# Cached latent attention of the sample group: four batches in four column tiles, and a page pool stored with its keys turned

## The chip, the core and the metric

The kernel is one program on one core of a Trainium2 chip. The number that counts is the device time of one execution in microseconds (us). TensorE (PE in the profile, PEld for its weight loads) multiplies, VectorE (DVE) and ScalarE (ACT) copy and reduce, GpSimd (POOL) and SyncE (SP) issue transfers here. An f32 matmul stands in the trace as two records, each with its own weight load.

## What is computed

One step of a two-layer decoder trunk for a prompt group (512 tokens) and a sample group (8 batches of 4 new tokens). The change is in the odd layer's latent attention of the sample group, which reads a paged cache of 16 pages of 128 keys for each batch:

```python
def mla_sample_attend(q_abs, q_pe, ckv, k_pe, pool_ckv, pool_kpe, page_table):
    past_ckv = pool_ckv[page_table].reshape(bd, past, c)          # 8 x 2048 x 256
    past_kpe = pool_kpe[page_table].reshape(bd, past, ROPE_DIM)   # 8 x 2048 x 32
    kc = jnp.concatenate([past_ckv, ckv], axis=1)
    kp = jnp.concatenate([past_kpe, k_pe], axis=1)
    sc = mla_scores(q_abs, q_pe, kc, kp)
    sc = jnp.where(kpos[None, :] <= qpos[:, None], sc, NEG)
    p = jax.nn.softmax(sc, axis=-1)
    return jnp.einsum('bhqj,bjc->bqhc', p.astype(kc.dtype), kc)
```

Each batch has 8 heads x 4 tokens = 32 query rows, so its scores are 32 rows by 2048 keys, with a contraction over 256 + 32 = 288 features.

## The kernel before

Most of the time goes to the dense panels (FFNs and projections, line 555), in each of which every weight panel is loaded by SP into `raw`, split by ACT and DVE into `w_hi` and `w_lo`, and multiplied. The order on each engine is written out by hand, with semaphores between them.

The odd layer runs its input panels, the prompt group's latent attention (`mla_score`, `mla_turn`, `mla_values`), then `sample()`, then `sample_out()` and the output panels (`mixer_out`). `mixer_out_begin` does the part of the first two output panels that needs no attention result; it stands behind the pages.

In `sample()` the 128 pages (8 batches x 16) go through TensorE one by one. A page arrives as 128 keys x 288 features (144 KB, `page_pool`). `turn_page` (line 862) turns it by three transposes against the identity, DVE and ACT copy the turned page from PSUM into `keys_t` in turns (lines 1608 and 1224), and `score_page` (line 875) multiplies it in three accumulating steps of 96 features with the stationary `qa` of that batch, 32 columns wide. Scores of batch b land in PSUM rows 32*(b%4) on, over banks 0 to 3. A score stands two pages behind its turn. Batch b-1's softmax runs beside batch b's pages: `sample_maxima` on DVE, four `Exp` on ACT (line 1232), `turn_probs` (line 906), and `page_values` (line 916), 16 accumulating matmuls of 256 columns against the pages as they came. The same loaded page serves both products.

`load_pages` issues the transfers: units of four pages, of which SP issues two of three and POOL the third. For each page the issuing engine reads the page number from the table (`value_load`, line 463), then issues one DMA (line 464). There are room and waits for 52 pages; the first 28 are loaded during the prompt group's attention.

## Time and profile before

| | us |
|---|---|
| median of 3 runs (lowest, highest) | 2413.91 (2412.71, 2418.8) |
| the profiled execution, span | 2412.8 |
| TensorE busy | 2344.1 (97%) |
| VectorE busy | 1085.6 (45%) |
| ScalarE busy | 754.7 (31%) |
| GpSimd busy | 232.4 (10%) |

The chain that ended last is 91% TensorE, of which 77% of the span is the panels' line 555, and lines 875 and 862, the page scores and page turns, are 4% and 2%. The span is the time from the first to the last instruction of one execution, so it can be set beside the median directly. In the views below, "x768" is a count of records, "idle before" is how long the engine had stood still, and the name behind "<-" is what it had waited for. The granted clock (PEclk) is 1.00 at 2.4 GHz and 0.50 at 1.2 GHz.

### The profile page before, as it was taken

What the parts mean: (1) busy time and instruction counts of PE and PEld (TensorE: products, weight loads), DVE (VectorE), ACT (ScalarE), POOL (GpSimd) and SP (SyncE); (2) the same over time, 40 slices, a digit from 0 to 9 for tenths busy, and PEclk for the clock granted to TensorE, in tenths of its full rate; (3) what the DMA queues carried; (4) which work ended last, traced back from release to release, by engine and by line L of the source; (5) the groups of instructions that cost most, each with busy time, mean ns of one, the idle gap of its engine ahead of it and who ended that gap; (6) DMA issues with size and microseconds to landing.
All of it is one profiled execution on the core that took longest, in us unless ns stands there. A gap on an engine that the chain in (4) does not pass through costs nothing.

```text
span 2412.8 us, 43405 instructions
## 1 busy us (share of the span) xinstructions
PE 2344.1 (97%) x17798; PEld 2200.5 (91%) x17798; DVE 1085.6 (45%) x1403; ACT 754.7 (31%) x1034; POOL 232.4 (10%) x201
## 2 busy tenths in 40 slices
PE   7999999998999999999999999988999989999997
PEld 7999999986999999999999999965666679999997
DVE  5432445455644244554334456664432345433443
ACT  5421222234344122244212222224422224522221
POOL 1001003000500000310000040400001021000002
PEclk9999999978999999999999999998999999999999
DMA  3243222320322222222222222232222112232222
GB/s 119 87 105 119 87 97 86 97 74 3 114 87 92 83 87 93 81 83 88 97 76 88 99 88 89 77 53 69 60 80 79 48 44 88 87 100 75 87 95 73
DMA packets 63131, 201.09 MB, mean 83 GB/s; under 512 B 8701, under 2 KB 20157, under 8 KB 62960
## 3 DMA queue, kind: packets, MB, share of 16 engines
q1 hardware_dynamic: 57776, 186.01, 23.8%
q0 software_dynamic: 5264, 13.79, 2.6%
q8 instruction: 66, 1.08, 0.2%
q14 instruction: 25, 0.20, 0.0%
HBM read 195.07 MB, written 5.71 MB: 83 GB/s over the span
## 4 chain that ended last, share of the span: by engine, by line
PE 91%; DVE 4%; ACT 2%; DMA 2%; issue 1%; DVEq 0%; SPq 0%; ACTq 0%
PE ps L555 77%; PE ps L875 4%; PE ps L862 2%; PE ps L916 2%; DMA raw<-down 1%; DMA raw<-w_uq 1%; DVE rinv L1288 1%; DVE w_lo L1278 1%; PE ps L791 1%; ACT prob L1093 1%; ACT p_mla L1190 0%; PE ps L643 0%; PE ps L804 0%; PE ps L642 0%; PE ps L906 0%
## 5 line engine op out<-in xcount | busy, mean ns | idle before, releaser
L555 PE MATMUL ps<-hx_hi,w_hi 128*128 128x272 f32 x3376 | 702.7, 289 | 15.5 <-DVE hx_lo L1299 13.1
L1026 ACT ACTIVATE w_hi<-raw 128x1024 fp32r<-128x1024 f32 (+2 forms) x299 | 334.6, 1119 | 1204.3 <-PE ps L555 1168.8
L555 PE MATMUL ps<-hx_hi,w_lo 128*128 128x272 f32 x3376 | 699.5, 289 | 0.0
L555 PE MATMUL ps<-hx_lo,w_hi 128*128 128x272 f32 x3376 | 696.9, 288 | 0.0
L555 PEld LDWEIGHTS ps<-hx_hi,w_hi 128*128 128x128 f32 x3376 | 531.7, 188 | 19.4 <-issue 14.3
L555 PEld LDWEIGHTS ps<-hx_lo,w_hi 128*128 128x128 f32 x3376 | 531.5, 189 | 0.0
L555 PEld LDWEIGHTS ps<-hx_hi,w_lo 128*128 128x128 f32 x3376 | 527.8, 189 | 0.0
L1278 DVE TENSOR_TENSOR w_lo<-raw,w_hi 128x1024 fp32r<-128x1024 f32 (+2 forms) x299 | 420.8, 1407 | 128.4 <-ACT w_hi L1026 128.1
L555 PE MATMUL ps<-hid_hi,w_hi 128*128 128x272 f32 x1408 | 291.9, 288 | 4.7 <-DVE w_lo L1278 4.7
L555 PE MATMUL ps<-hid_lo,w_hi 128*128 128x272 f32 x1408 | 291.6, 288 | 0.0
L555 PE MATMUL ps<-hid_hi,w_lo 128*128 128x272 f32 x1408 | 291.5, 288 | 0.0
L555 PEld LDWEIGHTS ps<-hid_hi,w_hi 128*128 128x128 f32 x1408 | 221.0, 189 | 4.9 <-issue 4.9
L555 PEld LDWEIGHTS ps<-hid_lo,w_hi 128*128 128x128 f32 x1408 | 221.0, 188 | 0.0
L555 PEld LDWEIGHTS ps<-hid_hi,w_lo 128*128 128x128 f32 x1408 | 220.9, 188 | 0.0
L1306 DVE SCALAR_TENSOR_TENSOR x<-ps,x 128x544 f32 (+1 forms) x80 | 57.9, 724 | 307.8 <-PE ps L555 307.8
L1323 DVE TENSOR_TENSOR up<-ps,rinv 128x544 f32<-128x544 f32 x88 | 63.8, 725 | 291.5 <-PE ps L555 291.5
L1320 DVE TENSOR_TENSOR gate<-ps,rinv 128x544 f32<-128x544 f32 x88 | 63.8, 725 | 232.8 <-PE ps L555 231.9
L1726 POOL TENSOR_TENSOR sumsq<-x 128x544 f32<-128x544 f32 x7 | 7.6, 1091 | 1337.5 <-DVE x L1306 1333.7
L1731 POOL TENSOR_TENSOR sumsq<-sumsq,square 128x544 f32<-128x544 f32 x49 | 113.0, 2306 | 3.8
L875 PE MATMUL ps<-keys_t,qa 96*32 96x128 f32 x768 | 107.5, 277 | 0.0
L875 PEld LDWEIGHTS ps<-keys_t,qa 96*32 96x32 f32 x768 | 73.7, 109 | 22.9 <-issue 22.9
L1608 DVE COPY keys_t<-ps 96x384 f32<-96x384 f32 x64 | 35.4, 554 | 103.7 <-PE ps L862 103.7
(280 smaller groups left out, 1955.8 us busy)
## 6 DMA issues: line engine op xcount, KB each, us to landing
raw<-gu SPq DMA_DIRECT2D x176, 512.0 KB, 3.4
raw<-down SPq DMA_DIRECT2D x64, 704.0 KB, 4.0
page<-page_pool SPq DMA_DIRECT2D x88, 144.0 KB, 2.5
raw<-odd_in SPq DMA_DIRECT2D x21, 512.0 KB, 3.4
raw<-even_in SPq DMA_DIRECT2D x14, 512.0 KB, 3.5
page<-page_pool POOLq DMA_DIRECT2D x40, 144.0 KB, 3.2
raw<-even_out SPq DMA_DIRECT2D x8, 512.0 KB, 3.4
raw<-odd_out SPq DMA_DIRECT2D x8, 512.0 KB, 3.5
```

The lines of the kernel that those rows point to most:

```text
L555: last = pe.matmul(acc[slot][0:m, a, 0:TH], w, r[:, t, a * TH:(a + 1) * TH], start=(begin and t == tiles[0] and one == 0), stop=(end and t ...
L791: pe.matmul(ps[:, i, 0:(i + 1) * P], qf[0:QK, h, i * P:(i + 1) * P], kf[0:QK, h, 0:(i + 1) * P], start=True, stop=True).then_inc(mla_score ...
L862: last = pe.transpose(ps[0:QK, page_bank[g], j * PAGE:(j + 1) * PAGE], pages[g % len(pages)][:, j * QK:(j + 1) * QK], ident[:])
L875: last = pe.matmul(ps_flat[r:r + NS, p * PAGE:(p + 1) * PAGE], qa[0:QK, j, b, :], keys_t[g % KT_SLOTS][:, j, :], start=(j == 0), stop=(j = ...
L916: pe.matmul(out, p_st[b % 2][:, p, :], pages[(b * PAGES + p) % len(pages)][:, 0:KV_LORA], start=(p == 0), stop=False)
L1026: act.activation(w_hi[slot][:, 0:cols], raw[slot][:, 0:cols], ACT.Copy).then_inc(w_hi_done, 1)
L1278: dve.tensor_tensor(w_lo[slot][:, 0:cols], raw[slot][:, 0:cols], w_hi[slot][:, 0:cols].bitcast(F32), ALU.subtract).then_inc(w_lo_done, 1)
L1306: dve.scalar_tensor_tensor(out=xm, in0=acc_of(slot), scalar=factor, in1=xm, op0=ALU.mult, op1=ALU.add)\
L1320: dve.tensor_tensor(halves(gate[:]), acc_of(n0 % 2), halves(rinv[:]), ALU.mult).then_inc(acc_read, 1)
L1323: dve.tensor_tensor(halves(up[:]), acc_of((n0 + 1) % 2), halves(rinv[:]), ALU.mult).then_inc(acc_read, 1)
L1608: dve.tensor_copy(keys_t[g % KT_SLOTS][:].rearrange("p j k -> p (j k)"), ps[0:QK, page_bank[g], 0:3 * PAGE])\
L1731: pool.tensor_tensor(sumsq[:], sumsq[:], square[:], ALU.add).then_inc(sumsq_step, 1)
```

## The change

The eight batches become two groups of four, and the four batches of a group are worked on together, batch b in column tile b (PSUM rows 32*b on).

- The pool is laid out twice. `pool_kt` holds each page with its features on the rows (96 rows of 3 x 128 elements, 144 KB), `pool_v` holds the latents as before without the rotary part (128 rows of 256 elements, 128 KB). The page table is stored in two orders to go with them.
- `turn_page` and the copies into `keys_t` are gone. `score_row(g, c)` multiplies four pages (512 keys) of each of four batches straight from `keys`: three feature steps, in each of which the four batches follow one another.
- `page_values(g)` takes one page of each of the four batches in turn, from `vals`. `score_new`, the masks, the maxima, the exponentials and `turn_probs` work on all 128 rows of a group at once.
- A unit is four pages: `load_keys` (32 units, all on SP, 8 slots) and `load_vals` (32 units, all on POOL, 9 slots). The four page numbers of a unit are read by one load. A slot of keys is free when its row of scores is done, a slot of values when its page is multiplied for all four batches. Two of the slots lie in `raw`, so SP loads the output panels from the third on only after the last page is used.
- `mixer_out_begin` moves from behind the pages to a place ahead of `page_values(1)`. Group 1's scores stand behind group 0's values.

```diff
+GROUPS = 2
+GB = DB // GROUPS
+ROWS = PAGES // 4
+K_SLOTS = 8
+V_SLOTS = 9
...
+        def page_numbers(eng, at):
+            return nc.values_load_multi_w_load_instructions(table[0:1, at:at + 4], engines=(eng.engine,), min_val=0, max_val=N_POOL - 1)[1]
+        def load_keys(eng, u):
+            if u == 0:
                 eng.wait_ge(table_landed, 16)
                 eng.wait_ge(q_done, HEADS)
                 eng.wait_ge(stored_conv, 32)
+            if u == 4:
+                eng.wait_ge(qa_done, 1)
+            if u == 6:
+                eng.wait_ge(w_lo_done, ODD_OUT + 2)
+            if u == 7:
                 eng.wait_ge(mla_scored, BLOCKS * HEADS)
+            if u >= K_SLOTS:
+                before = u - K_SLOTS
+                eng.wait_ge(scored[before % GB], before // (ROWS * GB) * (ROWS + 1) + before // GB % ROWS + 1)
+            for i, page in enumerate(page_numbers(eng, 4 * u)):
+                eng.dma_start(keys[u % K_SLOTS][:, i], d["pool_kt"][bass.ds(page, 1)].rearrange("a p j c -> (a p) j c"))\
+                   .then_inc(keys_landed[u % K_SLOTS], 16)
+        def load_vals(eng, u):
+            if u == 0:
+                eng.wait_ge(table_landed, 16)
+                eng.wait_ge(q_done, HEADS)
+            if u == 1:
+                eng.wait_ge(w_lo_done, ODD_OUT + 2)
+            if u == 2:
                 eng.wait_ge(qa_done, 1)
+                eng.wait_ge(mla_scored, BLOCKS * HEADS)
+            if u >= V_SLOTS:
+                before = u - V_SLOTS
+                for b in range(GB):
+                    eng.wait_ge(valued[b], before // PAGES * (PAGES + 1) + before % PAGES + 1)
+            for b, page in enumerate(page_numbers(eng, DB * PAGES + 4 * u)):
+                eng.dma_start(vals[u % V_SLOTS][:, b], d["pool_v"][bass.ds(page, 1)].rearrange("a p c -> (a p) c"))\
+                   .then_inc(vals_landed[u % V_SLOTS], 16)
...
+            for u in range(GROUPS * ROWS * GB):
+                load_keys(sp, u)
+            for b in range(GB):
+                sp.wait_ge(scored[b], GROUPS * (ROWS + 1))
+                sp.wait_ge(valued[b], GROUPS * (PAGES + 1))
...
+            def score_row(g, c):
+                if g == 0:
+                    pe.wait_ge(mla_exp, BLOCKS * HEADS)
+                else:
+                    pe.wait_ge(s_exp, c + 1)
+                for j in range(3):
+                    for b in range(GB):
+                        u = (g * ROWS + c) * GB + b
+                        if j == 0:
+                            pe.wait_ge(keys_landed[u % K_SLOTS], 64 * (u // K_SLOTS + 1))
+                        r = NS * b
+                        last = pe.matmul(ps[r:r + NS, c, :], qa[0:QK, j, g * GB + b, :], keys[u % K_SLOTS][:, :, j, :],
+                                         start=(j == 0), stop=(j == 2))
+                        if j == 2:
+                            last.then_inc(scored[b], 1)
+            def turn_probs(g):
+                for f in range(ROWS):
+                    pe.wait_ge(s_exp, g * (ROWS + 1) + f + 1)
+                    if f == 2 or f == 0 and g:
+                        pe.wait_ge(s_copied_act, 2 * g + f // 2)
+                    if f == 3 or f == 1 and g:
+                        pe.wait_ge(s_copied_dve, 3 * g + f // 2)
+                    for k in range(4):
+                        p = 4 * f + k
+                        last = pe.transpose(ps[:, 4 + f % 2, k * P:(k + 1) * P], p_s[:, p * PAGE:(p + 1) * PAGE], ident[:])
+                    last.then_inc(s_turned, 1)
+                pe.wait_ge(s_exp, (g + 1) * (ROWS + 1))
+                if g == 0:
                     pe.wait_ge(new_copied, 1)
                 else:
+                    pe.wait_ge(o_lat_done, g)
+                pe.transpose(ps[0:NS, 6, 0:P], p_s[:, PAGES * PAGE:PAGES * PAGE + NS], ident[:]).then_inc(s_turned, 1)
+            def page_values(g):
                 for p in range(PAGES):
+                    u = g * PAGES + p
+                    if p % 8 == 0:
+                        pe.wait_ge(s_copied_act, 2 * g + p // 8 + 1)
+                    if p % 8 == 4:
+                        pe.wait_ge(s_copied_dve, 3 * g + p // 8 + 1)
+                    pe.wait_ge(vals_landed[u % V_SLOTS], 64 * (u // V_SLOTS + 1))
+                    for b in range(GB):
+                        r = NS * b
+                        pe.matmul(ps[r:r + NS, 7, 0:KV_LORA], p_st[:, p, r:r + NS], vals[u % V_SLOTS][:, b, :], start=(p == 0), stop=False)\
+                          .then_inc(valued[b], 1)
+                pe.wait_ge(s_copied_dve, 3 * g + 3)
+                for b in range(GB):
+                    r = NS * b
+                    pe.matmul(ps[r:r + NS, 7, 0:KV_LORA], p_st2[:, r:r + NS], ckv_new[:], start=False, stop=True).then_inc(valued[b], 1)
             def sample():
+                turn_new()
+                for g in range(GROUPS):
+                    for c in range(ROWS):
+                        score_row(g, c)
+                    score_new(g)
+                    turn_probs(g)
+                    if g == GROUPS - 1:
+                        mixer_out_begin(ODD_OUT, CONV_TILES, CONV_PIECE + CT)
+                    page_values(g)
+                    turn_latents(g)
...
+                act.wait_ge(new_turned, 1)
+                act.activation(ckv_new[:], ps[0:NS, 6, 0:KV_LORA], ACT.Copy).then_inc(new_copied, 1)
+                for g in range(GROUPS):
+                    act.wait_ge(s_max, g + 1)
+                    if g:
+                        act.wait_ge(s_turned, g * (ROWS + 1))
+                    for c in range(ROWS):
+                        act.activation(p_s[:, c * 4 * PAGE:(c + 1) * 4 * PAGE], ps[:, c, :], ACT.Exp, bias=s_nmx[:, g:g + 1], scale=MLA_SCALE,
+                                       accum_out=s_sum[:, g, c:c + 1]).then_inc(s_exp, 1)
+                    act.activation(p_s[:, PAGES * PAGE:PAGES * PAGE + NS], s_new[:], ACT.Exp, bias=s_nmx[:, g:g + 1], scale=MLA_SCALE,
+                                   accum_out=s_sum[:, g, ROWS:ROWS + 1]).then_inc(s_exp, 1)
+                    if g:
+                        for b in range(GB):
+                            act.wait_ge(valued[b], g * (PAGES + 1))
+                    for f in (0, 2):
+                        act.wait_ge(s_turned, g * (ROWS + 1) + f + 1)
+                        act.activation(p_st[:, 4 * f:4 * f + 4, :].rearrange("p j r -> p (j r)"), ps[:, 4, :], ACT.Copy).then_inc(s_copied_act, 1)
...
+            def sample_maxima(g):
+                row = g * (ROWS + 1)
+                for c in range(ROWS):
+                    for b in range(GB):
+                        dve.wait_ge(scored[b], row + c + 1)
+                    dve.tensor_reduce(s_mx[:, g, c:c + 1], ps[:, c, :], AX, ALU.max)
+                for b in range(GB):
+                    dve.wait_ge(scored[b], row + ROWS + 1)
+                if g:
+                    dve.wait_ge(s_exp, row)
+                link(dve.tensor_tensor(s_new[:], ps[:, 7, KV_LORA:KV_LORA + NS], causal_s[:, g, :], ALU.add))
+                link(dve.tensor_reduce(s_mx[:, g, ROWS:ROWS + 1], s_new[:], AX, ALU.max))
+                link(dve.tensor_reduce(s_mx[:, g, ROWS + 1:ROWS + 2], s_mx[:, g, 0:ROWS + 1], AX, ALU.max))
+                dve.tensor_scalar(s_nmx[:, g:g + 1], s_mx[:, g, ROWS + 1:ROWS + 2], -MLA_SCALE, None, ALU.mult).then_inc(s_max, 1)
+            def sample_copies(g):
+                if g:
+                    for b in range(GB):
+                        dve.wait_ge(valued[b], g * (PAGES + 1))
+                for f in (1, 3):
+                    dve.wait_ge(s_turned, g * (ROWS + 1) + f + 1)
+                    dve.tensor_copy(p_st[:, 4 * f:4 * f + 4, :].rearrange("p j r -> p (j r)"), ps[:, 5, :]).then_inc(s_copied_dve, 1)
+                dve.wait_ge(s_turned, (g + 1) * (ROWS + 1))
+                dve.tensor_copy(p_st2[:], ps[0:NS, 6, 0:P]).then_inc(s_copied_dve, 1)
+            def sample_tokens(g):
+                for b in range(GB):
+                    dve.wait_ge(valued[b], (g + 1) * (PAGES + 1))
+                if g:
+                    dve.wait_ge(o_turned, g)
+                link(dve.tensor_reduce(s_rs[:, g, 0:1], s_sum[:, g, :], AX, ALU.add))
+                link(dve.reciprocal(s_rs[:, g, 1:2], s_rs[:, g, 0:1]))
+                dve.tensor_scalar(o_tok[:], ps[:, 7, 0:KV_LORA], s_rs[:, g, 1:2], None, ALU.mult).then_inc(o_tok_done, 1)
...
+            for u in range(GROUPS * PAGES):
+                load_vals(pool, u)
...
+    pool = np.concatenate([i["cache_mla_ckv"][0], i["cache_mla_kpe"][0]], -1)
+    a["pool_kt"] = pool.transpose(0, 2, 1).reshape(N_POOL, 3, QK, PAGE).transpose(0, 2, 1, 3)
+    a["pool_v"] = i["cache_mla_ckv"][0]
+    by_rows = i["page_table"].reshape(GROUPS, GB, ROWS, 4).transpose(0, 2, 1, 3)
+    by_pages = i["page_table"].reshape(GROUPS, GB, PAGES).transpose(0, 2, 1)
+    a["table"] = np.concatenate([by_rows.reshape(1, -1), by_pages.reshape(1, -1)], 1)
...```

**TensorE's order, scores.** Before, one period of one page in batch 2, with the score of a page two behind its turn (`page` is a page as loaded, `keys_t` a turned copy, `qa` the queries):

```order
L862 MATMUL ps<-ident_68,page33_182 96x128 [waits keys_copied0]
L862 MATMUL ps<-ident_68,page33_182 96x128 x2
L875 MATMUL ps<-keys_t1_170,qa_127 32x128 [waits keys_copied1]
L875 MATMUL ps<-keys_t1_170,qa_127 32x128 x2
L888 MATMUL ps<-ckv_115,qa_new_128 32x4 x2
L889 MATMUL ps<-kpe_116,qa_127 32x4
```

After, the first row of scores; a `keys` buffer holds four pages of one batch:

```order
L829 MATMUL ps<-ident_68,ckv_115 32x128 [waits mla_copied]
L829 MATMUL ps<-ident_68,ckv_115 32x128
L844 MATMUL ps<-keys0_146,qa_127 32x512 [waits keys_landed0,mla_exp]
L844 MATMUL ps<-keys1_147,qa_127 32x512 [waits keys_landed1]
L844 MATMUL ps<-keys2_150,qa_127 32x512 [waits keys_landed2]
L844 MATMUL ps<-keys3_145,qa_127 32x512 [waits keys_landed3]
L844 MATMUL ps<-keys0_146,qa_127 32x512
```

The transposes are gone, neighbouring matmuls are of different batches, and what they wait for is a transfer.

**TensorE's order, the end of the pages.** Before, the last values stand ahead of the output panels' first part:

```order
L916 MATMUL ps<-page22_163,p_st1_203 32x256
L916 MATMUL ps<-page23_164,p_st1_203 32x256
L917 MATMUL ps<-ckv_new_201,p_st2_176 32x256
...
L555 MATMUL ps<-mix_hi_72,w_hi1_57 128x272
L555 MATMUL ps<-mix_lo_73,w_hi1_57 128x272 x2
L555 MATMUL ps<-mix_hi_72,w_lo1_59 128x272 x2
...
L924 MATMUL ps<-ident_68,o_tok_175 128x128 [waits s_copied,o_tok_done]
```

After (`mix` and `w_hi` belong to the output panels):

```order
L879 MATMUL ps<-ident_68,p_s_163 32x128 [waits o_lat_done,s_exp]
L546 MATMUL ps<-mix_hi_72,w_hi1_57 128x272 [waits acc_read,w_lo_done,mix_done]
L546 MATMUL ps<-mix_hi_72,w_hi1_57 128x272
...
L892 MATMUL ps<-vals7_161,p_st_164 32x256 [waits vals_landed7,s_copied_act]
L892 MATMUL ps<-vals7_161,p_st_164 32x256 x3
...
L897 MATMUL ps<-ckv_new_165,p_st2_166 32x256 x3
L903 MATMUL ps<-ident_68,o_tok_149 128x128 [waits o_tok_done]
```

The panels' first part now stands between group 1's turned probabilities and its values.

**SP's order.** Before, one page has its own load of a page number; after, four pages share one, and the unit waits for a row of scores:

```order
L463 TENSOR_LOAD table [waits values_done]
L463 ISA x2
L464 ISA
L464 DMA page_177<-page_pool 128x288
L463 TENSOR_LOAD table
```

```order
L426 TENSOR_LOAD table [waits scored0]
L426 ISA x8
L444 ISA
L444 DMA keys_146<-pool_kt 96x384
L444 ISA
L444 DMA keys_146<-pool_kt 96x384
```

Three of four number loads are gone, and the wait comes every four pages.

## Rows read from the trace of the kernel before

**Rows 1.** Busy time by stretch: start:end, length, then each engine; clock, DMA, GB/s.

```profile
core 0: us, PE busy (x) PEld busy (x) DVE busy (x) ACT busy (x) POOL busy (x), PEclk, DMA share, GB/s
1711.00:1947.00 236.00, 230.58 (x1625) 151.56 (x1623) 67.38 (x151) 63.37 (x162) 13.41 (x25) 0.98 0.21 61
...
1704.00:1711.00 7.00, 3.85 (x21) 2.30 (x22) 2.74 (x9) 3.37 (x11) 3.22 (x6) 1.00 0.81 232
...
1937.00:1942.00 5.00, 4.67 (x11) 1.90 (x12) 0.00 (x0) 0.28 (x1) 0.00 (x0) 0.50 0.01 3
1943.00:1947.00 4.00, 4.00 (x20) 1.90 (x19) 0.00 (x0) 0.00 (x0) 0.00 (x0) 1.00 0.00 0
```

**Rows 2.** Groups by line and shape, 1706 to 1958: count, busy us, mean ns.

```profile
L875 PE MATMUL ps<-keys_t,qa 96*32 96x128 f32 x768 | 107.5, 277 | 0.0
...
L862 PE MATMUL ps<-ident,page 128*96 128x128 f32 x384 | 67.9, 286 | 0.3 <-DVE keys_t L1608 0.3
L916 PE MATMUL ps<-page,p_st 128*32 128x256 f32 x256 | 59.3, 392 | 0.8 <-ACT p_st L1242 0.8
...
L1573 DVE TENSOR_REDUCE mx<-ps 32x1 f32<-32x512 f32 x32 | 21.9, 685 | 2.4 <-PE ps L875 1.7
L1232 ACT ACTIVATE p_s<-ps,nmx 32x512 f32<-32x512 f32 x32 | 21.6, 675 | 5.7 <-DVE nmx L1583 5.3
```

**Rows 3.** TensorE in order of time, batch values and two pages: start, length.

```profile
1807.20 6.64 PE L916 MATMUL ps<-page,p_st 128*32 128x256 f32 x30
...
1815.55 0.53 PE L862 MATMUL ps<-ident,page 128*96 128x128 f32 x3
1816.01 0.84 PE L875 MATMUL ps<-keys_t,qa 96*32 96x128 f32 x6
1816.79 0.53 PE L862 MATMUL ps<-ident,page 128*96 128x128 f32 x3
```

**Rows 4.** TensorE in order of time, even layer, line 708, batches in four column tiles.

```profile
570.54 0.18 PEld L708 LDWEIGHTS ps<-k_cache,q_bd 128*32 128x32 f32 x8 [1.54 <-issue]
570.54 0.45 PE L708 MATMUL ps<-k_cache,q_bd 128*32 128x128 f32 x8
```

**Rows 5.** SP's and GpSimd's issues of pages; queue instructions: least/median/most ns.

```profile
1629.02 21.66 SPq L464 DMA_DIRECT2D page<-page_pool  x20
...
1705.46 0.54 POOL L464 DMA_DIRECT2D page<-page_pool  x1 [0.60 <-issue]
...
L463 SPq TENSOR_LOAD <-table x88: 262/269/487, 1628.0 to 1879.1; - x88
...
L463 POOLq TENSOR_LOAD <-table x40: 283/289/498, 1628.0 to 1874.7; - x40
```

**Rows 6.** DMA issues, 1640 to 1960: queue, count, KB, median us to landing.

```profile
page<-page_pool SPq DMA_DIRECT2D x78, 144.0 KB, 2.4
page<-page_pool POOLq DMA_DIRECT2D x32, 144.0 KB, 3.2
```

**Rows 7.** In order of time: prompt attention's end, batch 7's softmax, the tail.

```profile
1702.80 0.69 ACT L1190 ACTIVATE p_mla<-ps,nmx 128x512 f32<-128x512 f32 x1 [1.92 <-DVE nmx L1549]
...
1706.93 2.34 PE L815 MATMUL ps<-p_mla_t,v_mla 128*64 128x512 f32 x8 [0.78 <-ACT p_mla_t L1203]
...
1930.77 0.17 DVE L1580 TENSOR_TENSOR s_new<-ps,causal_s 32x4 f32<-32x4 f32 x1
...
1931.53 0.68 ACT L1232 ACTIVATE p_s<-ps,nmx 32x512 f32<-32x512 f32 x1 [3.07 <-DVE nmx L1583]
...
1934.20 0.28 ACT L1235 ACTIVATE p_s<-s_new,nmx 32x4 f32<-32x4 f32 x1
...
1947.58 0.15 DVE L1589 TENSOR_REDUCE rs<-sm 32x1 f32<-32x5 f32 x1 [16.08 <-PE ps L917]
...
1954.56 1.14 PE L954 MATMUL ps<-o_lat,w_uv 128*64 128x32 f32 x32 [0.58 <-DVE o_lat L1596]
...
1956.40 0.52 PE L555 MATMUL ps<-mix_hi,w_hi 128*128 128x272 f32 x2 [0.70 <-DVE mix_lo L1311]
```

More of the change, by code:

```diff
@@ L389, in decoder_step @@
         new_copied = sem("new_copied")
-        page_turned = sem("page_turned")
-        keys_copied = [sem(f"keys_copied{s}") for s in range(2)]
-        page_scored = sem("page_scored")
-        s_new_ready = sem("s_new_ready")
+        scored = [sem(f"scored{b}") for b in range(GB)]
         s_max = sem("s_max")
@@ L910, in page_values @@
-            def page_values(b):
-                r = NS * (b % 4)
-                pe.wait_ge(s_copied, b + 1)
-                out = ps[r:r + NS, 7, 0:KV_LORA]
-                for p in range(PAGES):
-                    pe.matmul(out, p_st[b % 2][:, p, :], pages[(b * PAGES + p) % len(pages)][:, 0:KV_LORA], start=(p == 0), stop=False)
-                pe.matmul(out, p_st2[:, b % 2, :], ckv_new[:, b, :], start=False, stop=True).then_inc(values_done, 1)
+                    pe.wait_ge(o_tok_done, g)
```

253 lines of the change are left out of this document (52 added, 201 removed).

## The prediction, made before the changed kernel had run

> **What bounds the kernel now.** I read the span first (2412.8 us, against a median of 2413.91: what I take off the one I take off the other), then the chain that ended last, which is 91% TensorE, and then busy time by stretch. The stretch to look at is 1711 to 1947, the sample group's pages: TensorE is busy 230.6 of 236 us at full clock while the transfers use 21% of the DMA engines [rows 1]. So TensorE's own instructions are the bound there, and the rest of the kernel is not touched by the change. In order of time one page costs 1.24 us (1815.55 to 1816.79): 0.46 for three turns and 0.78 for three f32 scores [rows 3]. 128 pages are 158.7 us. A batch's values are 30 records in 6.64 us, 0.22 us for each of 256 columns [rows 3], so 34 are 7.2 and eight batches 58 us. These two make 217 of the 236 us; the groups by line say the same [rows 2].
>
> **What goes and what comes on TensorE.** The page turns go (59 us), with their copies on DVE and ACT, which were beside it and free. What is left depends on whether column tiles run at once. The trace shows them elsewhere: in the even layer four batches follow each other into four column tiles, and eight 128-column records stand in 0.45 us, the last of which is 0.27 us long, so eight starts lie within 0.18 us; their weight loads too [rows 4]. One after the other they would take 8 x 0.11 = 0.86 us (half of 0.22 for half the columns). So four tiles run at once, two records of one matmul behind each other in their tile.
>
> The Trainium skill says otherwise for the loads: its page "TensorE: Matmul & The Clock Gate", section "Part 3: Packing small matmuls", has weight loads overlap running matmuls only when the row group differs, and here all four tiles share theirs. [Rows 4] speak against it, since loads and matmuls of one row group stand over each other there; by that rule the tiles would take turns, which is the second rival below.
>
> A row of scores is 6 records of 512 columns in each tile, 6 x 0.43 = 2.6, with its drain 2.7 us; a page of values of four batches is 2 x 0.22 = 0.45 us. Eight rows and 32 pages: 36 us instead of 217. The maxima, exponentials and turned probabilities now stand in the chain, since a group has no other group to hide it: 0.15 + 0.7 for the last maximum (685 ns for 512 columns [rows 2]), 0.8 for the new keys up to the first exponential (1930.77 to 1931.53), 3.05 us of exponentials (1931.53 to 1934.20 and 0.38 more), copy and waits 1.05 [rows 7]. A 128-row exponential takes 0.69 us [rows 7] where the 32-row one takes 0.675 [rows 2], so the width costs nothing. That is 1.65 + 4.1 us a group.
>
> **The transfers take over.** The pages are now loaded twice, 144 + 128 KB. SP issues a page every 1.12 us (20 in 21.66 us), GpSimd every 1.14 us (0.54 and 0.60 idle), of which the number load is 0.27 and 0.29 us [rows 5]. A unit of four with one number load instead of four is on SP 4 x 1.10 - 3 x 0.31 = 3.5 us, on GpSimd 4 x 1.14 - 3 x 0.32 = 3.6, and 3.8 from unit 9 on, where it has four waits to pass. Its upper bound is what they cost now, 4.4 and 4.8; the lower, 3.2 and 3.3, if the address work is shared too. Rows of 1,536 and 1,024 bytes instead of 1,152 I take at the same issue price. From issue to landing SP's take 2.4 us and GpSimd's 3.2 [rows 6]; behind the issue itself I put 2.5 and 2.65. The two queues would ask for 168 + 138 = 306 GB/s. In 1704 to 1711 they moved 232 GB/s at a DMA share of 0.81 [rows 1], an estimate of 286 at full share, so where both run they slow each other by a twentieth: 2 us in all.
>
> **The sum, in the time of the trace.** TensorE's last prompt record ends at 1709.3 [rows 7]; `turn_new` no longer waits for DVE and takes 0.5. Rows 0 and 1 (their keys are there) end at 1712.5 and 1715.2. Keys of row 2 go to slots freed by row 0: four units from 1712.5 to 1726.5, landed 1729.0. By now TensorE has stood still for 14 us, and where it had waited for batch 7's exponentials, some 4 us, the trace shows it at half clock right after: 11 records in 5 us at 0.50, then 20 in 4 us at 1.00 [rows 1]. So row 2 costs 5.3 and ends at 1734.3. Row 3's units are out at 1740.5, landed 1743.0, scored 1748.3. Plus 1.65 and 4.1: values of group 0 start at 1754.0.
>
> GpSimd, let go by the last prompt scores just ahead of 1702.8 as now [rows 7], has meanwhile put units 2 to 8 into its nine slots (1702.6 to 1727.8) and stands at unit 9 until page 0 is multiplied, 1754.9. Units 9 to 15: 7 x 3.8 = 26.6, landing 2.65, last products 1.6: 1785.8. Tokens and their turns 1.8. Rows 4 and 5 (keys there since 1771) at 5.3 and 4.0: 1792.9, 1796.9. Keys of row 6 from 1792.9 on, 14 + 2.5 + 5.3: 1814.7; row 7 four units later, 1828.7. GpSimd's units 16 to 24 are done at 1815.7 beside this.
>
> Now the move of `mixer_out_begin`: its 48 records of the panels stand ahead of group 1's values. Full clock they are 6 us, half clock 11; I take 9, and 1 for the probabilities ahead of them. Units 25 to 31 wait behind it, because their slots come free only by group 1's values. Values start at 1828.7 + 1.65 + 4.1 + 10 = 1844.4 and end 0.9 + 26.6 + 2.65 + 1.6 later, at 1876.1. What was 6 us behind the pages is thus no gain but stands in the same chain.
>
> The tail: before, from the last value (1947.5) 8.9 us to 1956.4, 6 of them `mixer_out_begin`; now tokens 1.0, turn 0.5, copy 0.6, `sample_out` 1.8 at half clock, splits 0.9 = 4.8: 1880.9, and 2.5 for the first panel records at half clock. SP's next panel is asked for at 1876.1 and landed some 5 us later, while the first two panels' second part keeps TensorE until after 1886; the split has time. So 1956.4 - 1883.4 = 73, less the 2 of shared engines: 71 us off 2413.9, **2343 us**.
>
> As a rule of thumb: 30 units lie in this chain (8 of keys, 7 of values, 8, 7), so a microsecond more for each costs 30.
>
> **Rivals.**
> - The issue costs what it costs now (4.4 and 4.8 us a unit). For: the issue instruction, not the number load, is most of it. 30 x 0.9 = 28 more: 2371. Chance 0.19.
> - The tiles take turns, and the change doesn't do what it says: 10.8 us a row, 1.8 a page, clock full since TensorE is then busier. Row 1 ends at 1731.4, row 3 1761.9, group 0's values 1801.2, row 7 1855.1, the last value 1901.6: 2365. [Rows 4] are against. Chance 0.1.
> - The clock stays full: rows 2.7, panels 6, no cold start, 15 us less: 2328. Against: pauses of 12 us behind nearly every row. Chance 0.15.
> - Slower than before: the moved bytes, not the issue, set the pace. Two layouts are 31 MB from 1702 on, where the stretch of before moved 61 GB/s [rows 1]. If a key or value unit moved at half the pace forecast (7.0 and 7.6 us), the chain would grow by 30 x 3.6 = 108 us: 2451. It is slower from 2.4 us more a unit, 5.9 and 6.2 us, that is under 100 GB/s a queue; 232 for two is seen, which leaves little. Chance 0.03.
>
> **How the numbers follow.** The forecast, 2343, with 10 us to each side for my estimates of panels, half clock and landing, has 0.5; 0.03 is left for an issue cheaper still (2319). The range reaches from the cheap issue to the sum of dear issue and the rest: 2315 to 2380. A measurement here can tell about 0.3%, 7 us, from no change. All cases but the last are faster by more: faster 0.96, same 0.01, slower 0.03.
>
> **What would show it.** The trace of after should have the last values around 1876 and the output panels by 1883; score records of four batches starting within 0.1 us of each other, a row in 2.7 or 5.3 us; SP's key issues 0.88 us apart; GpSimd silent from 1728 to 1755 and again from 1816 to 1845, and ending last before the values; the clock at 0.5 in most of the stretch; TensorE busy for less than a third of it. It is wrong if GpSimd's or SP's page takes 1.1 us, if rows take 10 us, or if TensorE, not a landed page, ends the waits.

## The result, and the profile after

The changed kernel takes **2343.6 us** (median of 4, 2342.1 to 2344.7), the kernel before 2415.3 in the same runs (2412.7 to 2418.8): a ratio of 0.970, 95% interval 0.969 to 0.972. The forecast was 2343 (2315 to 2380). The profiled execution took 2344.28 us, its span is 2342.6.

The rows of after that answer to those shown of before, busy time by stretch first (columns as in [rows 1]):

```profile
core 0: us, PE busy (x) PEld busy (x) DVE busy (x) ACT busy (x) POOL busy (x), PEclk, DMA share, GB/s
1707.00:1878.00 171.00, 93.28 (x593) 33.57 (x591) 12.03 (x28) 9.30 (x26) 61.03 (x114) 0.66 0.62 172
1718.00:1743.00 25.00, 16.96 (x58) 2.98 (x58) 0.85 (x2) 0.00 (x0) 5.62 (x11) 0.66 0.91 251
...
1837.00:1845.00 8.00, 8.00 (x56) 7.70 (x59) 0.60 (x2) 0.00 (x0) 0.00 (x0) 0.77 0.00 0
1845.00:1878.00 33.00, 11.02 (x124) 3.38 (x116) 0.00 (x0) 0.00 (x0) 15.02 (x28) 0.59 0.39 112
```

The pages took 236 us of a TensorE that was busy 98% of them. They now take 171, of which it is busy 93, much of that at the lower clock. The transfers went from a share of 0.21 to 0.62, and 0.91 from 1718 to 1743. That last is a mean of two parts: up to 1736 the share is 1.04 at 279 GB/s, so the DMA engines are full. From 1738, with GpSimd silent and its last early unit landed (1733.5), it is 0.59. The groups by line, 1700 to 1890, as in [rows 2]:

```profile
L844 PE MATMUL ps<-keys,qa 96*32 96x512 f32 x192 | 49.5, 824 | 28.3 <-DMA keys<-pool_kt 28.3
L892 PE MATMUL ps<-vals,p_st 128*32 128x256 f32 x256 | 23.8, 500 | 42.1 <-DMA vals<-pool_v 42.1
```

(L844 is the scores' line, L892 the values' line, L444 and L462 the issues of keys and of values.) The 235 us of three groups in [rows 2] are 73. What stands in their place is the right-hand column: 28 and 42 us in which TensorE waits for a landed unit. In order of time, rows 0 and 1 of group 0 and the wait for the first unit of row 2, then rows 2 and 3:

```profile
1707.59 5.36 PE L844 MATMUL ps<-keys,qa 96*32 96x512 f32 x48
...
1718.02 1.89 PE L844 MATMUL ps<-keys,qa 96*32 96x512 f32 x2 [5.07 <-DMA keys<-pool_kt]
1721.62 1.91 PE L844 MATMUL ps<-keys,qa 96*32 96x512 f32 x2 [1.71 <-DMA keys<-pool_kt]
1725.57 1.92 PE L844 MATMUL ps<-keys,qa 96*32 96x512 f32 x2 [2.04 <-DMA keys<-pool_kt]
1729.46 6.10 PE L844 MATMUL ps<-keys,qa 96*32 96x512 f32 x20 [1.97 <-DMA keys<-pool_kt]
...
1739.94 2.33 PE L844 MATMUL ps<-keys,qa 96*32 96x512 f32 x17 [1.32 <-DMA keys<-pool_kt]
```

48 records of 512 columns in 5.36 us are 0.11 each: four at once, since one alone needs 0.43 (e4 below). The first records of the four batches start 7 ns apart. The Trainium skill's rule that loads are hidden only across row groups ("TensorE: Matmul & The Clock Gate", "Part 3: Packing small matmuls") does not describe this row: four tiles of one row group did not take turns, and their weight loads of 0.11 us stand over running matmuls of the other tiles. The last two lines are the two clocks: 20 records in 6.10 us, 17 in 2.33. Row 2's units of keys land 3.6 to 4.0 us apart, behind an issue every 3.4 us; the last two of row 3, with GpSimd silent, land 1.5 and 2.4 us behind the one before. The issues, SP first and then GpSimd:

```profile
1715.27 15.71 SPq L444 DMA_DIRECT2D keys<-pool_kt  x20
...
1754.35 2.31 POOL L462 DMA_DIRECT2D vals<-pool_v  x4 [27.16 <-PE ps L892]
1758.54 2.31 POOL L462 DMA_DIRECT2D vals<-pool_v  x4 [1.89 <-issue]
1762.35 2.29 POOL L462 DMA_DIRECT2D vals<-pool_v  x4 [1.50 <-PE ps L892]
...
1847.64 2.29 POOL L462 DMA_DIRECT2D vals<-pool_v  x4 [32.62 <-PE ps L892]
```

SP puts 20 pages in 15.7 us, five units at just under 3.4 where they run on; before, 20 took 21.66 [rows 5]. GpSimd's units start 3.8 us apart once it has slots to wait for, and it is silent twice, for 27 and 33 us, until the first page of a group is multiplied. From issue to landing (page of the profile):

```profile
keys<-pool_kt SPq DMA_DIRECT2D x128, 144.0 KB, 3.7
vals<-pool_v POOLq DMA_DIRECT2D x128, 128.0 KB, 3.3
```

### The profile page after: what moved, and what is told of

Its sections match the earlier page's. It is cut to its first block, busy times and chain, and to the rows that moved or that the text cites. A ratio compares the mean times of both kernels' runs of the same rounds, so it can differ in the third digit from the quotient of the medians.

```text
span 2342.6 us, 41476 instructions
## 1 busy us (share of the span) xinstructions
PE 2204.5 (94%) x16722; PEld 2079.0 (89%) x16722; DVE 1029.6 (44%) x1279; ACT 699.7 (30%) x897; POOL 279.7 (12%) x289
## 4 chain that ended last, share of the span: by engine, by line
PE 86%; DVE 4%; DMA 3%; issue 3%; ACT 2%; SPq 2%; POOLq 1%; POOL 0%; DVEq 0%; ACTq 0%
PE ps L546 80%; DMA raw<-down 1%; SPq L444 1%; DVE rinv L1241 1%; PE ps L844 1%; DMA raw<-w_uq 1%; DVE w_lo L1231 1%; SPq L426 1%; PE ps L782 1%; POOLq L426 1%; DMA keys<-pool_kt 1%; ACT prob L1062 1%; ACT p_mla L1159 0%; PE ps L634 0%; PE ps L795 0%
## 5 line engine op out<-in xcount | busy, mean ns | idle before, releaser
L546 PE MATMUL ps<-hx_hi,w_hi 128*128 128x272 f32 x3376 | 702.7, 289 | 15.4 <-DVE hx_lo L1252 13.0
L546 PE MATMUL ps<-hx_hi,w_lo 128*128 128x272 f32 x3376 | 699.6, 289 | 0.0
L546 PE MATMUL ps<-hx_lo,w_hi 128*128 128x272 f32 x3376 | 696.9, 288 | 0.0
L546 PEld LDWEIGHTS ps<-hx_hi,w_hi 128*128 128x128 f32 x3376 | 531.8, 188 | 19.4 <-issue 14.4
L546 PEld LDWEIGHTS ps<-hx_lo,w_hi 128*128 128x128 f32 x3376 | 531.5, 189 | 0.0
L546 PEld LDWEIGHTS ps<-hx_hi,w_lo 128*128 128x128 f32 x3376 | 527.9, 189 | 0.0
L546 PE MATMUL ps<-hid_hi,w_hi 128*128 128x272 f32 x1408 | 292.2, 289 | 4.1 <-DVE w_lo L1231 4.1
L546 PE MATMUL ps<-hid_lo,w_hi 128*128 128x272 f32 x1408 | 291.9, 288 | 0.0
L546 PE MATMUL ps<-hid_hi,w_lo 128*128 128x272 f32 x1408 | 291.5, 288 | 0.0
L546 PEld LDWEIGHTS ps<-hid_hi,w_hi 128*128 128x128 f32 x1408 | 221.1, 189 | 4.4 <-issue 4.4
L546 PEld LDWEIGHTS ps<-hid_lo,w_hi 128*128 128x128 f32 x1408 | 221.3, 189 | 0.0
L546 PEld LDWEIGHTS ps<-hid_hi,w_lo 128*128 128x128 f32 x1408 | 221.0, 189 | 0.0
L462 POOL DMA_DIRECT2D vals<-pool_v x128 | 68.8, 538 | 208.5 <-issue 141.3
L1252 DVE SCALAR_TENSOR_TENSOR hx_lo<-x,gains,hx_hi 128x544 fp32r<-128x544 f32 (+1 forms) x48 | 78.8, 1647 | 0.1
L844 PE MATMUL ps<-keys,qa 96*32 96x512 f32 x192 | 49.5, 824 | 28.3 <-DMA keys<-pool_kt 28.3
## 6 DMA issues: line engine op xcount, KB each, us to landing
keys<-pool_kt SPq DMA_DIRECT2D x128, 144.0 KB, 3.7
vals<-pool_v POOLq DMA_DIRECT2D x128, 128.0 KB, 3.3
```

The costliest lines, as they stand in the source:

```text
L462: eng.dma_start(vals[u % V_SLOTS][:, b], d["pool_v"][bass.ds(page, 1)].rearrange("a p c -> (a p) c"))\
L546: last = pe.matmul(acc[slot][0:m, a, 0:TH], w, r[:, t, a * TH:(a + 1) * TH], start=(begin and t == tiles[0] and one == 0), stop=(end and t ...
L844: last = pe.matmul(ps[r:r + NS, c, :], qa[0:QK, j, g * GB + b, :], keys[u % K_SLOTS][:, :, j, :], start=(j == 0), stop=(j == 2))
L1252: dve.scalar_tensor_tensor(out=tile_of(hx_lo, m), in0=tile_of(x, m), scalar=gains[:, norm, bass.ds(m, 1)], in1=tile_of(hx_hi, m).bitcast(F ...
```

## Experiments

Each was run beside the kernel before, whose median was 2415.6, 2412.9 and 2415.0 us in the three sets (e1 to e4, e5 to e8, e9 to e11). Kernels of one set were on the same chip. The changed kernel's 2343.6 is from a set of its own, beside 2415.3 for the kernel before, so a difference between sets is good to some 3 us. The stage begins anywhere from 1704 to 1715 us in the profiled executions, by work ahead of it that no edit touches, so within a trace I count from the first record of group 0's scores ("the start"). From there to the end of the span the changed kernel takes 635.0 us (2342.6 less 1707.6).

**Does the page number load, or the issue, set the pace? (e3)**

```diff
-            for i, page in enumerate(page_numbers(eng, 4 * u)):
+            for i in range(4):
+                page = eng.value_load(table[0:1, 4 * u + i:4 * u + i + 1], min_val=0, max_val=N_POOL - 1)
```

and the same for the values.

> Edit: the changed kernel with one load of a page number for each page, as before, instead of one for four pages. Theory (the queues' issue sets the pace of 30 units in the chain): a unit costs 0.9 us more on SP (3.4 to 4.3) and on GpSimd (3.8 to 4.7), 30 x 0.9 = 27, 2371. Rival (the DMA engines set the pace where both queues run, units arrive 3.9 us apart already): only 0.4 to 0.8 us a unit is felt, in the stretches with one queue all of it: 2357.

Measured 2374.9 us (2372.0 to 2376.7), ratio 0.983 (0.981 to 0.985): 31.3 above the changed kernel. The first two lines below are the keys of row 2, 4.9 us apart instead of 3.9, the others GpSimd, 1.13 us a page instead of 0.95:

```profile
1727.26 1.91 PE L846 MATMUL ps<-keys,qa 96*32 96x512 f32 x2 [2.54 <-DMA keys<-pool_kt]
1732.20 1.92 PE L846 MATMUL ps<-keys,qa 96*32 96x512 f32 x2 [3.03 <-DMA keys<-pool_kt]
...
1769.48 0.54 POOL L464 DMA_DIRECT2D vals<-pool_v  x1 [0.61 <-issue]
1770.61 0.54 POOL L464 DMA_DIRECT2D vals<-pool_v  x1 [0.59 <-issue]
```

SP's unit went from 3.39 to 4.34 us and GpSimd's from 3.79 to 4.70, so 0.9 to 1.0 us more a unit cost 31 us, or 27 counted from the start (662.2 against 635.0). Either is the rule of thumb (30 units in the chain). The first rival of the prediction, 2371, would have been the time if one number load for four pages had not been cheaper.

**Do the column tiles run at once? (e4)**

```diff
-                        last = pe.matmul(ps[r:r + NS, c, :], qa[0:QK, j, g * GB + b, :], keys[u % K_SLOTS][:, :, j, :],
-                                         start=(j == 0), stop=(j == 2))
+                        last = pe.matmul(ps[0:NS, c, :], qa[0:QK, j, g * GB + b, :], keys[u % K_SLOTS][:, :, j, :],
+                                         start=True, stop=True)
```

and the same for the two value lines.

> Edit: the changed kernel with the scores and values of all four batches of a group written to the same 32 PSUM rows, each product a sum of its own, so that the four matmuls cannot run at once; the sums over feature steps and pages are left out by that and the output differs. Theory (four tiles at once are what makes rows 2.7 us at full clock): rows grow to about 10.5 us and pages of values to 1.8, of which the transfers hide most: 2365. Rival (tiles take turns already): no change, 2343.

Measured 2372.3 us (2369.5 to 2373.3), ratio 0.982 (0.980 to 0.984), 28.6 above the changed kernel. Rows 0 and 1:

```profile
1710.61 22.50 PE L844 MATMUL ps<-keys,qa 96*32 96x512 f32 x52
```

52 records in 22.5 us, 0.43 each against 0.11: without the four tiles each record stands alone. The theory said 2365 and the run was 7 us dearer; the rest of its prices I did not take apart. It also shows what rival two would have looked like: clock at 0.93 from 1707 to 1830, where the changed kernel has 0.65 (e9), and slower all the same.

**Issue or bytes? (e5, e6)** First the same bytes with a quarter of the issues and no number load:

```diff
-            for i, page in enumerate(page_numbers(eng, 4 * u)):
-                eng.dma_start(keys[u % K_SLOTS][:, i], d["pool_kt"][bass.ds(page, 1)].rearrange("a p j c -> (a p) j c"))\
+            if True:
+                eng.dma_start(keys[u % K_SLOTS][:].rearrange("p a j c -> p a (j c)"), d["pool_kt"][4 * u:4 * u + 4].rearrange("a p j c -> p a (j c)"))\
```

> Edit: the changed kernel with each unit of four pages loaded by one transfer from a fixed place in the pool, without page numbers; the same bytes in the same row lengths, but a quarter of the issues, and the pages are not those of the table, so the output differs. Theory (issue sets the pace): a unit falls from 3.4 to 3.9 us to what its bytes take, 590 KB at 276 GB/s or 2.1 us with one queue running; 30 units, 45 us less, 2299. Rival (the bytes set the pace): no change, 2340 to 2344.

Measured 2300.5 us (2297.4 to 2304.4), ratio 0.954 (0.952 to 0.956): 43 below the changed kernel, as the theory had it. Then the same issues with fewer bytes:

```diff
-                eng.dma_start(keys[u % K_SLOTS][:, i], d["pool_kt"][bass.ds(page, 1)].rearrange("a p j c -> (a p) j c"))\
+                eng.dma_start(keys[u % K_SLOTS][:, i, 0:2], d["pool_kt"][bass.ds(page, 1)].rearrange("a p j c -> (a p) j c")[:, 0:2])\
...
-                eng.dma_start(vals[u % V_SLOTS][:, b], d["pool_v"][bass.ds(page, 1)].rearrange("a p c -> (a p) c"))\
+                eng.dma_start(vals[u % V_SLOTS][:, b, 0:P], d["pool_v"][bass.ds(page, 1)].rearrange("a p c -> (a p) c")[:, 0:P])\
```

> Edit: the changed kernel with two of three key steps and half of the value columns loaded and multiplied: 160 instead of 272 KB a page, with the same number of issues; the rest of the product is left out. Theory (issue sets the pace): only the row's own time falls (1.7 us for each of the four late rows at half clock, 7 us) and what landing gains where both queues run, 5 us: 2331. Rival (the bytes set the pace): 30 units at 0.59 of 3.7 us, 45 us less, 2298.

Measured 2336.9 us (2334.5 to 2338.1), ratio 0.968 (0.967 to 0.970): 6.7 below. The two sets differ by 2.4 us in the kernel before, so by the ratios it is 5 us. Two fifths of the bytes, and a part of TensorE's work, buy 5 to 7 us; issues and number loads together, both of which e5 takes away, buy 40 to 43. Median landing, the two kernels' transfers from 1707 to 1830 (e6 above, e5 below):

```profile
keys<-pool_kt SPq DMA_DIRECT2D x96, 96.0 KB, 2.1
vals<-pool_v POOLq DMA_DIRECT2D x88, 64.0 KB, 2.3
```

```profile
keys<-pool_kt SPq DMA_DIRECT2D x24, 576.0 KB, 11.4
vals<-pool_v POOLq DMA_DIRECT2D x23, 512.0 KB, 9.4
```

So over the whole stage the issue is the bound, and the bytes are the longer landing where both queues run. In e5, with the issue gone, the DMA engines are the next bound: each unit is asked for in time and lands 9 to 11 us later.

**Where the panels of `mixer_out_begin` should stand (e1, e2, e9, e10)**

```diff
                 for p in range(PAGES):
+                    if g == GROUPS - 1 and p == 9:
+                        mixer_out_begin(ODD_OUT, CONV_TILES, CONV_PIECE + CT)
...
-                    if g == GROUPS - 1:
-                        mixer_out_begin(ODD_OUT, CONV_TILES, CONV_PIECE + CT)
```

> Edit: the changed kernel with mixer_out_begin moved from ahead of group 1's values to ahead of their tenth page. Theory (the end of the stretch is set by GpSimd's last seven units, which start when group 1's first pages are multiplied): values of group 1 start the 7.7 us earlier that the panel records took (1836.8 to 1844.5), the panels run while pages are on their way, so 2343.6 - 7.7 = 2336. Rival (TensorE's own work sets the end): the same work in another place, no change, 2343.

Measured 2344.7 us (2336.9 to 2345.1), ratio 0.970 (0.967 to 0.972). Three of four times are those of the changed kernel, one is the theory's. In the other direction, the panels behind the values where they stood before (only the order of two calls):

```diff
+                    page_values(g)
                     if g == GROUPS - 1:
                         mixer_out_begin(ODD_OUT, CONV_TILES, CONV_PIECE + CT)
-                    page_values(g)
```

> Edit: the changed kernel with mixer_out_begin back behind group 1's values, where it stood before. Theory: the last value comes 7.7 us earlier, and the panels' 6 to 8 us stand behind it, of which 1 us was a wait for the tokens anyway: 2342, within 2 us of the changed kernel. Rival (its new place hides it behind the transfers): slower by what it costs at the end, 6 to 8 us, 2350.

Measured 2347.2 us (2345.9 to 2350.8), ratio 0.972 (0.970 to 0.974): 3.6 above the changed kernel, between the two expectations, with intervals that overlap. Its profiled execution began the stage late, at 1715.0, and from there took 634.1 us, no more than the changed kernel's 635.0. Its trace has 8.9 us from group 1's last score to its first value, where the changed kernel has 16.0, and 8.5 us of panels behind the last value: so the panels cost about the same ahead of the values and behind them, as the first expectation had it. Since e1's times lay at both expectations, its kernel and the changed one ran again, in one set and five rounds.

> The changed kernel as it is, in the same call as e10, so that the two can be compared on one chip and over more executions. Both theories: 2344, within 2 either way of the 2343.6 measured first.

> The kernel of e1 (mixer_out_begin ahead of the tenth page of group 1's values) once more, beside e9. In e1 the 7.1 us between group 1's scores and its values were gained, but three of four times were 2344 to 2345 and one 2336.9. Theory: what e1 gained comes off the end, and the stage began late in three executions by accident; then the median here is 4 to 7 us under e9's, 2337 to 2340. Rival: loads stand behind the pages, so that the units of values land later when TensorE is 7 us ahead of them, and the gain is given back each time; then the median is within 2 us of e9's.

e9: 2344.7 us (2341.1 to 2351.0), ratio 0.972 (0.970 to 0.973). e10: 2341.7 us (2340.0 to 2343.5), ratio 0.970 (0.969 to 0.972). The difference, 3.0 us, is between the two theories, and the intervals overlap. The traces say where the rest is. First e9: the last steps of group 0's row 3, then the end of group 1's turns and its first values.

```profile
1741.54 2.33 PE L844 MATMUL ps<-keys,qa 96*32 96x512 f32 x17 [1.30 <-DMA keys<-pool_kt]
...
1837.36 0.42 PE L879 MATMUL ps<-ident,p_s 128*32 128x128 f32 x1
1844.19 4.09 PE L892 MATMUL ps<-vals,p_st 128*32 128x256 f32 x72
```

The same places in e10:

```profile
1740.14 4.47 PE L844 MATMUL ps<-keys,qa 96*32 96x512 f32 x17 [2.37 <-DMA keys<-pool_kt]
...
1838.83 0.42 PE L879 MATMUL ps<-ident,p_s 128*32 128x128 f32 x1
1839.18 4.72 PE L894 MATMUL ps<-vals,p_st 128*32 128x256 f32 x72
```

From the last turn to the first value 6.8 us became 0.35, a gain of 6.5 us, and it was not given back by the loads (first to last value 33.6 and 34.0). But the last 17 steps of group 0's row 3, which the edit does not touch, took 4.47 us at half clock instead of 2.33. They did so in both profiled executions of this kernel, and in neither of the changed one's. Counted from the start, `sample_out` comes 3.2 us earlier in e10 than in e9: 6.5 gained, 2.3 lost in group 0's rows, 1.0 in small change. Whether the edit moves the clock's spells or this is chance, these runs don't settle. What the two traces show is a gain of 6.5 us where the edit is made and 3.2 at the end; by the times alone the 3.0 is not clear of noise.

**Is the half clock worth a filling? (e7)**

```diff
+            def fill(bank, n):
+                for _ in range(n):
+                    pe.matmul(ps[:, bank, :], ident[:], ckv[:, 0, 0:SEQ], start=True, stop=True)
...
+                        if j == 0 and c > 1:
+                            fill(5, 3)
...
+                    if p > 8:
+                        fill(4, 3)
```

> Edit: the changed kernel with idle work on TensorE: three 512-column f32 matmuls into a free bank (2.6 us at full clock) ahead of each batch's first step in the third and fourth row of scores, and ahead of each page of values from the tenth on. Theory (half clock costs 2.6 us in each row that ends a wait, 15 us in all with panels and tail): the clock stays at 1.0 and 12 us of that come back, less overshoot: 2332. Rival (the clock does not matter, the transfers hide it): no change or slower by the idle work, 2343 to 2350.

Measured 2345.9 us (2344.1 to 2350.6), ratio 0.972 (0.970 to 0.974), no gain. The last unit of row 2, and the fillings around it:

```profile
1726.36 2.84 PE L835 MATMUL ps<-ckv,ident 128*128 128x512 f32 x6
1729.13 2.76 PE L851 MATMUL ps<-keys,qa 96*32 96x512 f32 x18
1731.82 2.84 PE L835 MATMUL ps<-ckv,ident 128*128 128x512 f32 x6
```

The clock did rise: 18 records in 2.76 us, where the changed kernel needs 6.10 for 20. But the next filling of 2.8 us stands ahead of row 3, and there is one ahead of every unit and page from then on: group 0's rows took 42.3 us from the start, against 35.1, and `sample_out` came 178.1 us after it, against 174.1. The last unit of row 3 had landed at 1739.3, and TensorE reached it at 1745.8, behind two more fillings: a filling that is still ahead in TensorE's order when the data lands is paid in full.

**Both queues in the order of need (e8, e11).** SP is silent while values are short, and GpSimd while keys are. e8 takes e1's kernel and deals the units from the eighth of keys on, in the order in which TensorE wants them, in turn to SP and GpSimd (each slot also gets a landing semaphore for each queue, which the excerpt leaves out):

```diff
+        MERGED = ([("k", 7)] + [("v", u) for u in range(2, 6)] + [("k", u) for u in range(8, 16)] + [("v", u) for u in range(6, 9)]
+                  + [("k", u) for u in range(16, 20)] + [("v", u) for u in range(9, 16)] + [("k", u) for u in range(20, 24)]
+                  + [("v", 16), ("v", 17)] + [("k", u) for u in range(24, 32)] + [("v", u) for u in range(18, 32)])
...
+        def load_half(eng, half):
...
+            for kind, u in MERGED[half::2]:
+                (load_keys if kind == "k" else load_vals)(eng, u)
...
-            for u in range(GROUPS * ROWS * GB):
+            for u in range(7):
                 load_keys(sp, u)
+            load_half(sp, 0)
```

> Edit: as e1_mid, and the units of keys and values from the eighth on are dealt out in turn to SP and GpSimd, in the order in which TensorE needs them, so both queues issue whichever kind is next. Theory (each phase waits for one queue while the other stands still): units come at 2.1 us, the DMA engines' own pace, instead of 3.4 to 3.9: values of group 0 end near 1760, of group 1 near 1815: 2280. Rival (the DMA engines' pace with both queues is no better than one queue's issue): 2330.

Measured **2297.9 us** (2294.1 to 2299.6), ratio 0.953 (0.951 to 0.954). It beats both kernels: 46 us below the changed one, 115 below the one before. It is 18 above the theory. Busy time by stretch, as for after above, and the pages of group 0's values:

```profile
1718.00:1743.00 25.00, 17.25 (x87) 6.51 (x85) 2.82 (x8) 4.17 (x12) 12.54 (x24) 0.57 0.97 275
...
1750.74 0.64 PE L916 MATMUL ps<-vals,p_st 128*32 128x256 f32 x8 [2.63 <-DMA vals<-pool_v]
1752.15 1.08 PE L916 MATMUL ps<-vals,p_st 128*32 128x256 f32 x8 [0.77 <-DMA vals<-pool_v]
1755.80 1.94 PE L916 MATMUL ps<-vals,p_st 128*32 128x256 f32 x16 [2.56 <-DMA vals<-pool_v]
1758.70 1.08 PE L916 MATMUL ps<-vals,p_st 128*32 128x256 f32 x8 [0.97 <-DMA vals<-pool_v]
1761.44 1.08 PE L916 MATMUL ps<-vals,p_st 128*32 128x256 f32 x8 [1.66 <-DMA vals<-pool_v]
1764.10 1.08 PE L916 MATMUL ps<-vals,p_st 128*32 128x256 f32 x8 [1.58 <-DMA vals<-pool_v]
```

The same seven pages in after:

```profile
1760.50 1.08 PE L892 MATMUL ps<-vals,p_st 128*32 128x256 f32 x8 [5.06 <-DMA vals<-pool_v]
...
1782.04 1.08 PE L892 MATMUL ps<-vals,p_st 128*32 128x256 f32 x8 [2.59 <-DMA vals<-pool_v]
```

The seven pages (one record of 16 is two) come 2.2 us apart, 1750.7 to 1764.1, instead of 3.6, and group 0's values start 36.6 us after the start and not 43.3. The DMA engines stand at 0.97 of their time. To tell whether they are the new bound, e11 takes e6's cut of the bytes on top of e8.

> Leaves out a part of the computation, as e6 did: two of the three key steps are loaded and multiplied, and half of the value columns (160 of 272 KB a pair of units), on top of e8's dealing of the units to both queues. e8's trace shows the DMA engines busy 0.97 at 275 GB/s in 1718 to 1743. Theory: with the issue shared by two queues the bytes are what is left to bound, so the same cut that gave 6.7 us in e6 gives more here: 2298 less some 18 of landing and 5 of TensorE's shorter rows, 2275. Rival: e8 is still bound by the issue, 28 units a queue of 3.5 us (98 us from 1707, to 1805, and the last pages after that), and only TensorE's shorter rows are saved: 2293.

Measured 2281.6 us (2278.4 to 2284.3), ratio 0.945 (0.943 to 0.946), 16.3 below e8 (19 by the ratios, since the two are of different sets). The same cut was worth 5 to 7 in e6, so bytes weigh more than twice as much here, if less than the 23 of the theory. e11's DMA share in 1718 to 1743 is 0.66, which points to the issue of two queues as its bound; that was not tested. In e8 the two stand close behind each other; how much each is worth was not taken further apart.

## Why the prediction was right, point by point

- **TensorE's part** (row 2.7 us, four tiles at once): rows 0 and 1 took 5.36 us against 5.4. e4 shows that the tiles carry it.
- **The issue** (SP 3.5 us a unit, GpSimd 3.6 and then 3.8, 30 units in the chain): 3.39, 3.64 and 3.79. e3 shows both the price of the number loads and the rule of 30 us for 1. Within a unit SP's issues stand 0.50 us apart; the 0.88 that was to be seen is the mean with the number load, measured 0.85.
- **GpSimd's two silences** (1728 to 1755, 1816 to 1845): the resumptions are at 1754.4 and 1847.6.
- **A sign that did not come true:** TensorE was to be busy for less than a third of the stage, and it was busy for 93 of 171 us, 55%. The sum had 36 us for scores and values, at full clock, and their records cover 73. The mean clock was 0.66, and of each late unit the first two records run alone in their tile, 1.9 us at half clock. Most of this lies in waits for the next unit and costs nothing in the chain.
- **The chain in time:** values of group 0 were forecast to start at 1754.0 and end at 1785.8, group 1's 1844.4 and 1876.1; they were 1750.9, 1784.1, 1844.6 and 1879.2. The panels start at 1884.4 and are at half clock for 4.0 us, which is 2.0 lost: 1886.4, against 1883.4 in the sum, plus 2 for shared engines, 1885.4.

That last agreement is better than its parts. Against the sum, in us (the forecast's stage is 1709.8 to 1883.4, without the 2 for shared engines):

| part | forecast | measured | difference |
|---|---|---|---|
| start of the rows | 1709.8 | 1707.6 | -2.2 |
| rows 0 to 3 | 38.5 | 35.1 | -3.4 |
| maxima, exponentials, turns, group 0 | 5.75 | 8.2 | +2.4 |
| values, group 0 | 31.8 | 33.2 | +1.4 |
| tokens, rows 4 to 7 | 42.9 | 44.5 | +1.6 |
| turns and panels, group 1 | 15.75 | 16.0 | +0.2 |
| values, group 1 | 31.7 | 34.6 | +2.9 |
| tail with its half clock | 7.3 | 7.2 | -0.1 |
| sum of the differences | | | +2.8 |

The steps that were mis-sized:

- **Start.** The half-clock spell far ahead of the stage was shorter in this execution (1635.9 to 1649.5, before 1635.4 to 1652.5); the forecast had no reason for it, and the other profiled executions start anywhere from 1704 to 1715. It is luck of 2 us.
- **Row 3 at half clock.** The sum had 5.3 us for it; its last 17 records ran at full clock in 2.33. The low clock was right for the stretch as a whole (0.66 on average), not for each place. The rival that had it full throughout is out.
- **The softmax.** I had 5.75 us from the last score to the first value. It is 8.2: from the first exponential to the values 5.8 and not 4.1, and 2.4 ahead of it, not 1.65. In the 2.4 stand 1.4 us of products with the new keys of four batches behind the last score (to 1744.1), which the sum left out. In the 5.8 the two halves of the turned probabilities wait for each other:

```profile
1745.09 0.69 ACT L1186 ACTIVATE p_s<-ps,s_nmx 128x512 f32<-128x512 f32 x1 [36.73 <-DVE s_nmx L1536]
...
1747.93 0.69 DVE L1545 COPY p_st<-ps 128x512 f32<-128x512 f32 x1 [2.87 <-PE ps L872]
...
1748.06 0.60 ACT L1195 ACTIVATE p_st<-ps 128x512 f32<-128x512 f32 x1
...
1748.81 1.94 PE L872 MATMUL ps<-ident,p_s 128*128 128x128 f32 x8 [0.92 <-ACT p_st L1195]
1750.54 0.42 PE L879 MATMUL ps<-ident,p_s 128*32 128x128 f32 x1
```

  The exponentials run to 1748.1. Only then is the first half copied (to 1748.7), and the second half's turns, 1.9 us, stand behind that copy. The sum had the copies beside the exponentials. The second half's turns also ran at a clock of 0.50, in both groups: eight in 1.94 us, where ten of the prompt group's took 1.28 at 1.00. By that, an estimate, the clock accounts for some 0.9 of the 1.7 us, and the wait for the copies for the rest. In all the softmax is 2.4 us over the sum in group 0 and 2.2 in group 1.
- **Landing and shared engines.** The estimate of 286 GB/s for full engines was near: 279 at a share of 1.04 from 1718 to 1736. What was missing is a queue that builds up. The two queues ask for more than that (306 in the sum), so each unit of keys lands later behind its issue than the one before, until GpSimd stops. In group 0 this is over in time: the issue of row 3's last unit ends at 1737.7, and it lands at 1739.9, 2.2 us later. In group 1 it is not: the last issue of keys ends at 1819.0, and the unit lands at 1824.6, 5.6 us later, where the sum had 2.5. Those 3 us, less 1.4 for a cheaper last row, are the +1.6.
- **GpSimd's last units.** The +1.4 and +2.9 of the two groups' values are not landing, which was shorter than the sum had it where GpSimd runs alone: 1.9 us behind the last issue and not 2.65. The time from the first value to the end of GpSimd's last issue was 29.2 us in group 0 (1750.9 to 1780.1) and 30.7 in group 1 (1844.6 to 1875.2), where the sum had 27.5; the last products took 2.1 and not 1.6. Of the excess, 1.1 and 0.7 us lie ahead of GpSimd's first issue, 3.5 and 3.1 us behind the first value, where the sum had 0.9 and its 1.5 for the number load. In group 1 another 2.1 us is one pause behind the first issue of a unit:

```profile
1859.19 0.54 POOL L462 DMA_DIRECT2D vals<-pool_v  x1 [1.65 <-issue]
1861.84 1.73 POOL L462 DMA_DIRECT2D vals<-pool_v  x3 [2.11 <-issue]
```

  The same pause of 2.1 us stands in the same unit in e1, e2, e3, e6, e7, e9 and e10, so it is not chance. What GpSimd does in it, no run shows.
- **The panels** were put at 9 + 1 us and took 8.0 (1836.55 to 1844.56). That hid the softmax's error in group 1.

So the mechanism and the main term, 30 units at their issue price, are right and were tried from both sides: dearer issues in e3, cheaper ones in e5 (which also loads its pages from neighbouring places, so not all of its gain need be the issue). That the last digits agree is a sum of errors that cancel.

The rival cases: dear issue (2371) is excluded by the row of issues and made by e3 (2375); tiles in turn (2365) by the first row of scores and made by e4 (2372); full clock (2328) by the granted clock. The slower one, bytes set the pace, would have needed under 100 GB/s a queue; both together moved 251 on average. The engines were full for a part of each group, but e6 shows the bytes to be worth 5 to 7 us in all.

## What to carry to other kernels

When a change takes an engine's work away, count what is left in the chain per unit of the next resource, here 30 issues, and price one microsecond of it: that one number foretold what dearer issues would cost (e3). Then look where that resource stands idle: the queues took turns, each waiting for slots while the other was short, and dealing the same transfers in the order of need brought 46 us more (some 3 of them from the place of the panels), with no operation less. Where two queues together ask for more than the DMA engines give, follow how late the last transfer lands that something waits for: 2.2 us behind its issue in group 0 here, 5.6 in group 1. Of a softmax that comes into the chain, follow each copy's releaser before adding up busy times.
